# Encoder trunk on one core: LayerNorms cut into two token halves, products at their ends computed half by half, three weight buffers, blocks unrolled

## What is computed

```python
def swiglu(u, w_in, w_out):
    gate, up = jnp.split(u @ w_in, 2, axis=-1)
    return (jax.nn.silu(gate) * up) @ w_out

for l in range(DEPTH):
    mod = (sc @ w_ada[l] + b_ada[l]).reshape(B, 3, 3, 1, D_MODEL)
    shift, scale, gate = mod[:, :, 0], mod[:, :, 1], 1.0 + mod[:, :, 2]
    h = swiglu(x * (1.0 + scale[:, 0]) + shift[:, 0], w_ff_in[l, 0], w_ff_out[l, 0])
    x = layer_norm(DEEP_ALPHA * x + 0.5 * gate[:, 0] * h, ln_g[l, 0], ln_b[l, 0])
    u = x * (1.0 + scale[:, 1]) + shift[:, 1]
    h = even_mixer(u, ...) if l % 2 == 0 else s5_mixer(u, ...)
    x = layer_norm(DEEP_ALPHA * x + gate[:, 1] * h, ln_g[l, 1], ln_b[l, 1])
    h = swiglu(x * (1.0 + scale[:, 2]) + shift[:, 2], w_ff_in[l, 1], w_ff_out[l, 1])
    x = layer_norm(DEEP_ALPHA * x + 0.5 * gate[:, 2] * h, ln_g[l, 2], ln_b[l, 2])
```

## Time and profile before

| quantity | value |
|---|---|
| runs | 2902.56, 2906.2, 2915.89 us |
| median | 2906.2 us |
| span of the profiled execution | 2909.0 us |
| its device time | not listed apart from the span; the span is 2.8 us over the median and inside the three runs |
| mean granted TensorE clock | 0.923 |
| busy | TensorE 89%, VectorE 53%, ScalarE 24%, GpSimd 3% |
| HBM traffic | 86 GB/s mean over the span |

### The profile page before, as it was taken

The page is one execution under the profiler, slowest core; times in us unless marked ns, Lnnn a source line. Parts: engine busy times, 40 slices in busy tenths (PEclk is TensorE's granted clock), DMA queues, the critical chain, the costliest instruction groups (busy, mean ns, idle before and its releaser), DMA issues.

```text
span 2909.0 us, 43873 instructions
## 1 busy us (share of the span) xinstructions
PE 2595.3 (89%) x18258; PEld 2481.8 (85%) x18258; DVE 1532.1 (53%) x2371; ACT 710.0 (24%) x784; POOL 88.0 (3%) x116
## 2 busy tenths in 40 slices
PE   5999998986779788999999799999667897999996
PEld 5999997984668557999999799999567796999996
DVE  4768665634542434665574676335888345333333
ACT  2122123333111422321112422113312213221222
POOL 0000000100000000100000100000000001000000
PEclk9999999996885789999999899999779898999998
DMA  6445432130000111243343143222100021222211
GB/s 262 159 148 200 172 118 85 61 76 0 1 1 4 53 44 58 102 166 118 123 155 117 69 164 108 94 81 73 66 1 1 16 73 44 81 71 94 84 57 51
DMA packets 39568, 250.89 MB, mean 86 GB/s; under 512 B 5312, under 2 KB 5888, under 8 KB 15792
## 3 DMA queue, kind: packets, MB, share of 16 engines
q1 hardware_dynamic: 26784, 172.25, 17.2%
q0 software_dynamic: 11248, 73.97, 7.5%
q10 hardware_dynamic: 1440, 3.32, 0.3%
HBM read 246.09 MB, written 3.43 MB: 86 GB/s over the span
## 4 chain that ended last, share of the span: by engine, by line
PE 58%; DVE 10%; ACT 1%; issue 1%; POOL 0%; DMA 0%; DVEq 0%; ACTq 0%
PE ps L272 49%; PE ps L432 2%; PE ps L411 1%; PE ps L1946 1%; DVE x L516 1%; DVE tb L1709 1%; DVE be L1709 1%; DVE ln_rstd L512 1%; PE ps L1164 1%; DVE wm L1709 1%; PE ps L1153 1%; PE ps L1161 1%; PE ps L1334 1%; DVE uf L469 1%; DVE ta L1709 1%
## 5 line engine op out<-in xcount | busy, mean ns | idle before, releaser
L272 PE MATMUL ps<-u_hi,w_hi 128*128 128x288 f32 x3392 | 735.2, 299 | 75.5 <-POOL u_lo L481 46.5
L272 PE MATMUL ps<-u_lo,w_hi 128*128 128x288 f32 x3392 | 732.9, 298 | 0.0
L272 PE MATMUL ps<-u_hi,w_lo 128*128 128x288 f32 x3392 | 732.4, 298 | 0.0
L272 PEld LDWEIGHTS ps<-u_hi,w_hi 128*128 128x128 f32 x3392 | 553.2, 191 | 79.3 <-issue 77.2
L272 PEld LDWEIGHTS ps<-u_lo,w_hi 128*128 128x128 f32 x3392 | 553.3, 191 | 0.0
L272 PEld LDWEIGHTS ps<-u_hi,w_lo 128*128 128x128 f32 x3392 | 553.1, 191 | 0.0
L247 DVE TENSOR_TENSOR w_lo<-w_raw,w_hi 128x2048 fp32r<-128x2048 f32 x176 | 403.2, 2292 | 224.1 <-ACT w_hi L242 223.6
L242 ACT ACTIVATE w_hi<-w_raw 128x2048 fp32r<-128x2048 f32 x176 | 337.0, 1915 | 549.8 <-PE ps L272 519.3
L540 DVE SCALAR_TENSOR_TENSOR ada_out<-ada_w,c_act 128x1024 f32<-128x1024 f32 x272 | 317.0, 1221 | 43.1 <-DMA ada_w<-in_w_ada 26.3
L272 PE MATMUL ps<-h_lo,w_hi 128*128 128x288 f32 x1600 | 338.2, 296 | 0.0
L272 PE MATMUL ps<-h_hi,w_hi 128*128 128x288 f32 x1472 | 321.1, 300 | 5.0 <-DVE h_lo L1709 5.0
(11 more groups left out here) (346 smaller groups left out, 2120.8 us busy)
## 6 DMA issues: line engine op xcount, KB each, us to landing
w_raw<-in_w_in SPq DMA_DIRECT2D x88, 1024.0 KB, 4.9
ada_w<-in_w_ada POOLq DMA_DIRECT2D x64, 1024.0 KB, 5.0
w_raw<-in_w_out SPq DMA_DIRECT2D x32, 768.0 KB, 4.1
w_raw<-in_w_out SPq DMA_DIRECT2D x32, 640.0 KB, 3.8
w_raw<-in_w_mix_in SPq DMA_DIRECT2D x10, 1024.0 KB, 4.9
ada_w<-in_w_ada SPq DMA_DIRECT2D x8, 1024.0 KB, 25.9
w_raw<-in_w_mix_out SPq DMA_DIRECT2D x4, 1024.0 KB, 4.7
w_raw<-in_w_glu SPq DMA_DIRECT2D x4, 1024.0 KB, 4.7
```

Source lines behind the costliest of these rows:

```text
L272: m = pe.matmul(out[:, a, :], w, mv[:, a, :], start=start and n_ == 0, stop=stop and n_ == 2)
```

## The change

**Norms by token half.** `ln_vector`, `ln_scalar`, `late_mean`, `square_sums` each run for half a = 0 (tokens 0 to 287) and then a = 1. Half tiles of 288 columns take the place of tiles of 576, so the norm has twice the instructions. All sixteen `u_lo` half tiles are made by GpSimd. The sample columns are in half 1 only.

**Both ends of a norm.** `tail` takes the last two output blocks: half 0 of both, then half 1 of both, with the late means and square sums of half 0 put into half 1's matmuls. `head` takes the first two input blocks: half 0 of both, then half 1 of both, with half 1's late means after k = 1 and its square sums before the second block. `mix_out` and `s5_out` are eight blocks of one tile now, with their means of tiles 0 to 5 ahead of later blocks.

**Weights.** Ring of three (NS = 3); `w_lo` is written over `w_raw`, so a load of block g waits until the product of block g - 3 is done. Splits cover only the block's width (1536, 1280, 1024 columns where it is narrower than 2048), and stand ahead of block b's evacuation instead of behind it.

**Unrolled.** All block loops are written out. TensorE's program has 16,724 matmuls where it had 7,204.

**Other.** The last of the S5 parameter stages runs behind norm 3 instead of ahead of it; `y` is stored as sixteen half tiles.

```diff
+    def head(pe, name, n):
+        g, hi, lo = first[name], tile_of(u_hi), tile_of(u_lo)
+        pe.wait_ge(s_wlo, g + 1)
+        if n:
+            pe.wait_ge(s_ra, 2 * n)
+        for k in range(KD):
+            wait_u_half(pe, n, 0, k)
+            half_step(pe, g, 0, 2, KD, hi, lo, 0, k)
+            if n and k == 1:
+                late_mean(pe, n - 1, 1)
+        if n:
+            square_sums(pe, n - 1, 1)
+        pe.wait_ge(s_wlo, g + 2)
+        for k in range(KD):
+            half_step(pe, g + 1, 1, 2, KD, hi, lo, 0, k)
+        for b in range(2):
+            for k in range(KD):
+                if b == 0:
+                    wait_u_half(pe, n, 1, k)
+                mm = half_step(pe, g + b, b, 2, KD, hi, lo, 1, k)
+            mm.then_inc(s_blk, 1)
+
+    def tail(pe, name, n, kk, mov_hi, mov_lo):
+        g, hi, lo = first[name] + KD - 2, tile_of(mov_hi), tile_of(mov_lo)
+        for b in range(2):
+            pe.wait_ge(s_wlo, g + b + 1)
+            pe.wait_ge(s_evac, g + b - 1)
+            mean_tile(pe, KD - 4 + b, 0)
+            mean_tile(pe, KD - 4 + b, 1)
+            for k in range(kk):
+                mm = half_step(pe, g + b, b, 1, kk, hi, lo, 0, k)
+            mm.then_inc(s_bh, 1)
+        for k in range(kk):
+            if k == 4:
+                late_mean(pe, n, 0)
+            if k == 5:
+                square_sums(pe, n, 0)
+            mm = half_step(pe, g, 0, 1, kk, hi, lo, 1, k)
+        mm.then_inc(s_blk, 1)
+        for k in range(kk):
+            mm = half_step(pe, g + 1, 1, 1, kk, hi, lo, 1, k)
+        mm.then_inc(s_blk, 1)
...
+    def ln_vector(dve, name, n):
+        g_next = done(name)
...
+        dve.wait_ge(s_bh, 2 * n + 1)
+        residual_part(dve, n, KD - 2, 0, HALF, 0).then_inc(s_ra, 1)
+        split_lo(dve, g_next)
+        dve.wait_ge(s_bh, 2 * n + 2)
+        residual_part(dve, n, KD - 1, 0, HALF, 0).then_inc(s_ra, 1)
+        for a in range(2):
+            if a:
+                for b in range(KD - 2, KD):
+                    dve.wait_ge(s_blk, first[name] + b + 1)
+                    residual_second_half(dve, n, b)
+            dve.wait_ge(s_mean, 2 * n + a + 1)
+            for k in range(KD):
+                dve.tensor_tensor(half(x, k, a), half(x, k, a), pair(1)[:, a, :], ALU.subtract).then_inc(s_cen, 1)
+            if a:
+                split_lo(dve, g_next + 1)
+            dve.wait_ge(s_std, 2 * n + a + 1)
+            chains["dve"].step(dve.reciprocal(ln_rstd[:, a, :], ln_std[:, a, :]))
...
+            for k in range(KD):
+                dve.tensor_tensor(half(x, k, a), half(x, k, a), ln_rstd[:, a, :], ALU.mult).then_inc(s_nrm, 1)
+                if a and n < NMOD - 1 and k:
+                    u_sample(dve, n + 1, k - 1)
...
     def u_gpsimd(pool, n):
-        for k in range(0, KD, 2):
-            u_low_tile(pool, n, k, s_up)
+        for a in range(2):
+            for k in range(KD):
+                pool.wait_ge(s_uhi, ln_count(nth(n), a, k))
+                pool.tensor_tensor(half(u_lo, k, a), half(u_f32, k, a), half(u_hi, k, a).bitcast(F32),
+                                   ALU.subtract).then_inc(s_up, 1)
...
+    def stream_load(sp, name, src):
+        for b in range(dict(STREAM)[name]):
+            g = first[name] + b
+            if g >= NS:
+                sp.wait_ge(s_blk, g - NS + 1)
+            sp.dma_start(w_raw[:, g % NS, 0:WIDTH[g]], src(b)).then_inc(s_raw[g % NS], 16)
```

More of the change, by code:

```diff
@@ L184, in trunk @@
     s_mod1 = sem("second_modulation_row_summed")
[L185 removed]
+    s_raw = [sem(f"weight_block_loaded_{n}") for n in range(NS)]
     s_whi = sem("weight_hi_ready")
@@ new lines, in three_half, with weights, tile_of, product @@
+    def three_half(pe, out, wh, wl, mh, ml, start, stop):
+        m = None
+        for n_, (w, mv) in enumerate(((wh, mh), (wh, ml), (wl, mh))):
+            m = pe.matmul(out, w, mv, start=start and n_ == 0, stop=stop and n_ == 2)
+        return m
+    def weights(g, tiles, kk):
+        return [w[:, g % NS, 0:kk * tiles * P].rearrange("p (k m c) -> p k m c", k=kk, m=tiles) for w in (w_hi, w_lo)]
+    def tile_of(t):
+        return t if callable(t) else (lambda k: t[:, k, :])
+    def product(pe, name, b, tiles, kk, mov_hi, mov_lo, ready=None):
+        g, hi, lo = first[name] + b, tile_of(mov_hi), tile_of(mov_lo)
+        wh, wl = weights(g, tiles, kk)
+        pe.wait_ge(s_wlo, g + 1)
+        if g >= 2:
+            pe.wait_ge(s_evac, g - 1)
+        for m_ in range(tiles):
+            for k in range(kk):
+                if ready is not None and m_ == 0:
+                    ready(k)
+                mm = three(pe, pair(2 * (b % 2) + m_), wh[:, k, m_, :], wl[:, k, m_, :],
+                           halves(hi(k)), halves(lo(k)), k == 0, k == kk - 1)
+        mm.then_inc(s_blk, 1)
@@ L364, in ffn_vector @@
             if s == 0:
[L365 to L373 removed]
+                gate_vector(dve, site)
+                for b in range(KD):
+                    split_lo(dve, first[f"out{f}0"] + b + 2)
+                    residual(dve, f"out{f}0", site, b)
+                    if f == 0:
+                        ada_unit(dve, SEGS[0][1], b // 2, b % 2)
@@ L453, in u_scalar, with half, mean_tile, late_mean @@
-    def u_scalar(act, n):
+        for b in range(KD - 2):
+            split_lo(dve, g1 + b + 2)
+            residual(dve, name, n, b)
+            if b < len(stages):
+                stages[b]()
+        ln_vector(dve, name, n)
+        if stages:
+            stages[6]()
+    def half(t, k, a):
+        return t[:, k, a * HALF:a * HALF + HALF]
+    def mean_tile(pe, k, a):
+        return pe.matmul(pair(1)[:, a, :], mean_w[:, :], half(x, k, a), start=k == 0, stop=k == KD - 1)
+    def late_mean(pe, n, a):
+        if a == 0:
+            pe.wait_ge(s_ra, 2 * n + 2)
+        else:
+            pe.wait_ge(s_evac, done(LN_NAMES[n]))
+        for k in range(KD - 2, KD):
+            m = mean_tile(pe, k, a)
+        m.then_inc(s_mean, 1)
@@ L1457, in mix_tensor @@
     def mix_tensor(pe):
-        body, count = product(pe, "mix_in", 2, KD, u_hi, u_lo, ready_first=u_ready(pe, 1))
-        blocks_loop(pe, count, body, start=1)
+        head(pe, "mix_in", 1)
+        for b in range(2, 10):
+            product(pe, "mix_in", b, 2, KD, u_hi, u_lo)
         norms_tensor(pe)
@@ L1465, in mix_tensor, with out_scalar @@
         pe.wait_ge(s_ol, 9)
-        body, count = product(pe, "mix_out", 2, KD, u_hi, u_lo)
-        blocks_loop(pe, count, body)
-    def out_scalar(act, name):
-        g0 = first[name]
-        def body(i, r, _):
-            act.wait_ge(s_blk, g0 + r + 1 + 2 * i)
-            split_hi(act, g0 + 2, r, i)
-        blocks_loop(act, 4, body)
+        out_tensor(pe, "mix_out", 1, KD, u_hi, u_lo)
+    def out_scalar(act, name, n):
+        for b in range(KD - 2):
+            split_hi(act, first[name] + b + 2)
+            if n == 1 and b == 2:
+                conditioning_scalar(act, s_in2, True)
+        ln_scalar(act, name, n)
     def mix_scalar(act):
```

521 lines of the change are left out of this document (216 added, 305 removed).

## The result

| | before | changed |
|---|---|---|
| median | 2906.68 us (2902.56 to 2915.89) | 2817.07 us (2807.01 to 2834.76) |
| ratio | | 0.9691, 95% interval 0.9654 to 0.9727 |
| span of the profiled execution | 2909.0 | 2813.7 |
| granted clock, mean | 0.923 | 0.930 |

A forecast was written before the change was run, and what follows sets the result against it. TensorE bounds the kernel, losing time mainly in pauses around the norms. Gains at norms, start, `mix_in` and attention sum to 91.1 us; 2906.2 less that gives 2815 us, range 2797 to 2850.

The forecast's parts named there:

- Norms 1, 2 and 4: At these norms, each half's vector work runs beside the other half's products; gains 19.0, 18.5 and 20.0 us.
- Norm 0 with `mix_in` and its end: Norm 0 gains 16.4 us; at the end of `mix_in`, a third buffer saves 5.5 of TensorE's 7.64 us wait.
- T0: Start of the forecast's count at a norm: the end of the third-last output block.
- Norm 3: S5 stage moves behind the last residual, the S5 parameters that follow end no earlier; gain 0.2 us.
- Norm 5: Last norm, no head to hide behind, but half 0 done earlier and half 1's chain shorter; gain 4.8 of 33.2 us.
- Start: Kernel start: half 0 has no sample columns, so TensorE begins at about 50.5 instead of 55.14; gain 4.7 us.
- Attention: A split where the rotary step waits for VectorE becomes half as wide and earlier; gain 2.0 us (0 to 2.3).
- Half 1's exclusion: VectorE and GpSimd blocking each other at half 1's `u_lo`: 2.1 us stall; full effect some 13 us off the sum.
- merely shifted: Rival at the norms: TensorE stands at both halves' square sums, about half of 74 us hidden; 2860 us, chance 0.11.
- Instruction fetch: Rival in TensorE's unrolled blocks: new instruction packets halt it, 2952 us at 1.5 us each; slower 0.05, gain cancelled 0.02.
- The second half stalls: Rival at four norms: half 1's tiles or weight splits come late, 8 us more each; 2847 us, chance 0.20.

The follow-up runs named there:

- e3: Changed kernel with last two output blocks and first two input blocks computed whole, norm still in halves; 2926.47 us, ratio to before 1.0051.
- e1: The changed kernel run again, nothing edited; 2826.16 us, ratio 0.9703.
- before again: The kernel before run again, nothing edited, for a second profile; 2912.36 us, ratio 1.0003.
- e6: e5 plus the low split of the third `mix_in` block ahead of VectorE's wait for the convolution state; 2807.11 us, ratio 0.9651.
- e5: Changed kernel with the last S5 parameter stage inside norm 3, where VectorE waits for half 1's root; 2813.86 us, ratio 0.9665.
- e2: Kernel before with all block and load loops written out, nothing else; 2916.47 us, ratio 1.0009.
- e4: Changed kernel with only the first two input blocks computed whole, the output end half by half; 2891.71 us, ratio to before 0.9932.
- e9: e6 with the first k tile of each block computed half by half; 2823.31 us, ratio 0.9710.
- e10: e6 with each whole block computed half after half; 2815.70 us, ratio 0.9682.
- e7: Changed kernel with half 1's `u_lo` shared: GpSimd makes even tiles, VectorE odd ones; 2830.15 us, ratio 0.9722.
- e12: The kernel of e6 run again, nothing edited; 2817.69 us, ratio 0.9695.

## Why the prediction was right, and where it was not

The mechanism was right: e3 against e1 shows that the interleaving carries more than the whole net gain (91.3 us of 80.9, the rest of the change costing 10.4). The prediction's terms against the two kernels in profiles without quick networks (before again less changed again, 80.9 us for the forecast's 91.1):

- **Norms 1, 2 and 4:** 18.9, 18.8 and 20.0 us; forecast 19.0, 18.5, 20.0. In norm 4's 20.0 the quick gated unit has 1.3 us; the first profile, without it, gives 19.5. At norm 2 TensorE's marks of half 0 held to 0.3 us, and the end to 0.3; between them two errors offset. Half 1's square sums began 1.4 us late, since TensorE waited 1.0 us for half 1's means where the schedule said that nothing waits, and the stall on `u_lo` was 0.3 us where it said 2.1.
- **Norm 0 with `mix_in` and its end:** 19.7 for 16.4 + 5.5 (by its own words, 1.7 less than norm 2's 74.8, norm 0 before is 73.1 and not 72.8, which would make the 16.4 a 16.8). The ends are as forecast (norm 0's head ends about 56 us after its T0, and TensorE waits 2.1 us for the first q/k squares where it waited 7.64). What is missing is inside: VectorE reaches the split of the third `mix_in` block behind a wait for the convolution state, which I had not followed. TensorE waited 1.3 us in the first profile and 1.6 in the second; e6 moved the split.
- **Norm 3:** 2.5 us lost for 0.2 gained. The step said that the parameters end no earlier. It missed that gain and bias (4.0 us) and then the whole stage (8.9 us) now follow norm 3's last multiplication on VectorE. e5 shows it.
- **Norm 5:** 2.6 (4.4 in the first profile, with the higher clock at the end) for 4.8, a term that the prediction did not add up from its parts. The chain there has VectorE finish half 0's multiplication (3.04 us) before half 1's residual (1.12), with no head to cover it; no run tried another order.
- **Start:** 2.6 (3.3) for 4.7. TensorE began at 51.6, not 50.5. I had taken GpSimd's half tile at 0.7 us, its price alone, and had not asked what VectorE does beside it. The first two `u_lo` half tiles take 1.88 and 2.83 us, and the other fourteen 0.79 or 0.80. The first two run beside VectorE's two `w_lo` splits (from 48.48 to 53.57), of which the second takes 2.88 us instead of 2.29. TensorE waits for both tiles (4.0 us to the first, 0.9 to the second). It is the exclusion that the prediction weighed for half 1, at a place where it did not look for it.

```profile
L557 POOL TENSOR_TENSOR u_lo<-u_f,u_hi x16: 787/796/2830, 49.5 to 64.1; 128x288 fp32r<-128x288 f32 x16
```
```profile
L262 DVE TENSOR_TENSOR w_lo<-w_raw,w_hi x2: 2292/2586/2881, 48.5 to 50.7; 128x2048 fp32r<-128x2048 f32 x2
```

- **Attention:** the wait named did shrink by 2.0 (6.9 to 4.9 us), but the whole stretch is 0.8 shorter. TensorE's 1618 records are busy for 338.8 us at a granted clock of 0.69, against 336.4 at 0.70 in before again, which would account for the rest; no run tests it.

The structural sum was 10 us too high, and quick networks, which no row of before showed, put back 8 us each: 16 in the first profile, 0 in the second. The first set's median, 2817, is where the changed kernel is with two of them; the repeat's, 2826, where it is with one. So the forecast was met as closely as it was by chance.

**Half 1's exclusion** was the place where the rule was weighed. The line L557 (`u_lo`) and VectorE's L593 and L542 in norm 2 (ns min/median/max):

```profile
L557 POOL TENSOR_TENSOR u_lo<-u_f,u_hi x16: 794/828/1122, 1558.0 to 1583.7; 128x288 fp32r<-128x288 f32 x16
```
```profile
L593 DVE TENSOR_TENSOR x<-x,ln_rstd_tail x8: 444/452/1110, 1574.7 to 1580.8; 128x288 f32<-128x288 f32 x8
```
```profile
L542 DVE TENSOR_SCALAR u_f<-x,u_scale,u_shift x8: 303/792/845, 1575.5 to 1581.9; 128x64 f32<-128x64 f32 x8
```

VectorE's instructions go from 0.45 to 1.11 (one of eight) and from 0.30 to 0.8 us when they meet GpSimd, and the last tile is done at 1584.6, T0 + 48.5 (forecast 48.8). The Trainium skill (SBUF — State Buffer, Who interferes with whom) says just this of L593, which has two SBUF inputs, against a GpSimd instruction that reads SBUF, and the trace agrees. L542 has one tensor input and slows too, so two inputs are not the only case here. TensorE waited only 0.3 us for `u_lo` at norm 2, for the 2.1 forecast: its third quarter began about 1 us later than scheduled, and it then asks for a tile every 0.8 us while they come 0.9 to 1.0 us apart. The 13 us that the rule's full effect would have cost did not come.

**The rivals.** The chain was not merely shifted: the waits at the square sums are 0.6 us in the tails of norms 0, 1, 2 and 4, and TensorE has half 1's means 1.0 to 1.4 us late. Instruction fetch fell by e2. The second half stalls by 0.3 to 1.4 us, not 8.

## What to carry to other kernels

Where an engine pauses for a chain of reductions across engines, cut the chain and the products on both its sides along an axis on which they are independent, and let each half's chain run beside the other half's products: cutting the chain alone gained nothing (e3, 1.0051), the interleaving 91 us. Count a pause of TensorE at more than its length, since the small matmuls in it and the restart run at a lower clock (0.71 and 0.53 in e4): the head was worth 11.5 to 14.1 us a norm where the schedule had said 9 to 11. An exclusion between two engines has to be looked for at every place where both run, not only at the one that was being weighed: here it held up the start. Before a total is believed because it meets the forecast, split it by stretches of a second profile of the same kernel; here 16 us of the gain and 5 us of loss were drawn, not earned.

## What the runs showed of the hardware that was not expected

- A long run of matmuls of 288 columns, two PSUM banks in turn, goes at 0.1333 or at 0.1300 us each, at a granted clock of 1.00 either way. It held for whole networks (some 300 us), changed between executions of one kernel, began where the order of the matmuls changes behind the head, and ended at the first float32 means (output blocks of 7.99 us for 60 from there on). Of 28 networks behind a half-by-half head with blocks in the two-bank order, 12 were quick; of the 20 behind whole heads and the 8 with e9's and e10's block order, none. A half-by-half head is not needed for it: `mix_in` was quick in one profile (e6), and the four blocks of the gated unit, which follow no head, in three (e1, e7, e12). What sets it stays open: no run turned it on at will.
- Half after half into one bank runs at 0.1325 to 0.1327 us a matmul in every network, `mix_in` and gated unit of e10's profile.
- GpSimd's 128x288 subtraction took 1.88 and 2.83 us beside VectorE's 128x2048 subtractions at the start, and 0.80 us behind them.
- In the attention part, where TensorE has gaps all along, the granted clock over the stretch differs between executions of one kernel (0.72 and 0.70), which is worth 6 us.
